# Dividing attention outputs instead of probabilities, in the second and third layer of a fused three-layer kernel

## The reference, cut to what matters

```python
# second layer, per query (256 tokens are one block, so only the own block is seen, causally)
s_own = einsum('bcgrd,bkgd->bcgrk', qc, k_own) * scale
p = masked_softmax(s_own, m_own)          # exp(s - max) / max(sum, 1e-30)
o = einsum('bcgrk,bkgd->bcgrd', p, v_own)
out = (o * silu(z)) @ w_out

# third layer, per block of heads
s = where(valid, q k^T * scale + bias, NEG)
p = softmax(concat([s, sink_col]))[..., :span]      # heads 0-7; heads 8-15 have no sink
o = einsum('bgrqk,bkgd->bqgrd', p, v)
mixed = concat([rms_norm_2(o_a, out_norm_a), rms_norm_2(o_b, out_norm_b)])
x = x + gate1 * (mixed @ w_out)
```

## Time and profile before

| | us |
|---|---|
| median of 3 runs | 1329.05 (1327.18 to 1329.94) |
| the profiled execution | 1329.2 |
| its span in the profile | 1327.9 |
| PE busy / DVE busy / ACT busy in the span | 1263.0 / 1040.0 / 596.9 |

### The profile page before, as it was taken

The page is one execution under the profiler, slowest core; times in us unless marked ns, Lnnn a source line. Parts: engine busy times, 40 slices in busy tenths (PEclk is TensorE's granted clock), DMA queues, the critical chain, the costliest instruction groups (busy, mean ns, idle before and its releaser), DMA issues.

```text
span 1327.9 us, 21963 instructions
## 1 busy us (share of the span) xinstructions
PE 1263.0 (95%) x8283; PEld 1096.5 (83%) x8283; DVE 1040.0 (78%) x2322; ACT 596.9 (45%) x1105; POOL 233.4 (18%) x180
## 2 busy tenths in 40 slices
PE   5988999988999899999999999999999999999997
PEld 5677865676597569999999999999988888888886
DVE  5587896687667878999878888899877777777776
ACT  1434693546342624566554444444443343333432
POOL 0354000360000004688940000000000000000001
PEclk9999999999999989999999999999999999999999
DMA  9877631867578327355544444454566565655553
GB/s 356 294 236 264 240 137 64 291 213 248 186 276 340 112 72 277 136 193 194 175 160 143 159 144 159 144 159 144 161 215 195 191 193 194 196 192 191 193 194 104
DMA packets 92382, 256.82 MB, mean 193 GB/s; under 512 B 9472, under 2 KB 16896, under 8 KB 91904
## 3 DMA queue, kind: packets, MB, share of 16 engines
q1 hardware_dynamic: 59728, 195.91, 44.2%
q10 hardware_dynamic: 32560, 59.66, 12.6%
HBM read 254.47 MB, written 1.06 MB: 192 GB/s over the span
## 4 chain that ended last, share of the span: by engine, by line
PE 72%; DVE 14%; POOL 5%; DMA 3%; ACT 3%; issue 3%; SPq 1%; DVEq 0%; ACTq 0%; POOLq 0%
PE bank L1729 27%; PE bank L1736 26%; PE bank L693 6%; PE bank L2016 4%; PE bank L1123 3%; DVE arena L434 2%; DVE arena L970 2%; PE bank L801 2%; DMA arena<-in_w_in 2%; POOL head_ms L824 2%; DVE u_lo L685 1%; DVE arena L1010 1%; DVE v_lo L685 1%; DMA arena<-in_ada_w 1%; SPq L303 1%
## 5 line engine op out<-in xcount | busy, mean ns | idle before, releaser
L1729 PE MATMUL bank<-h_hi,u_hi 128*128 128x256 f32 x632 | 179.8, 285 | 1.1 <-ACT arena L1854 1.1
L1729 PE MATMUL bank<-h_lo,u_hi 128*128 128x256 f32 x632 | 176.1, 279 | 0.0
L1729 PE MATMUL bank<-h_hi,u_lo 128*128 128x256 f32 x632 | 176.1, 279 | 0.0
L1729 PEld LDWEIGHTS bank<-h_hi,u_hi 128*128 128x128 f32 x632 | 118.8, 188 | 1.3 <-issue 1.3
L1729 PEld LDWEIGHTS bank<-h_hi,u_lo 128*128 128x128 f32 x632 | 119.4, 189 | 0.0
L1729 PEld LDWEIGHTS bank<-h_lo,u_hi 128*128 128x128 f32 x632 | 119.4, 189 | 0.0
L2112 ACT ACTIVATE u_hi<-raw 128x1024 fp32r<-128x1024 f32 x64 | 68.0, 1062 | 104.3 <-PE bank L1736 104.3
L2112 ACT ACTIVATE v_hi<-raw 128x1024 fp32r<-128x1024 f32 x64 | 68.0, 1062 | 101.1 <-PE bank L1736 101.1
L2173 POOL TENSOR_SCALAR raw<-raw 128x1024 f32<-128x1024 f32 x1 | 2.8, 2812 | 624.4 <-DMA raw<-in_final_g 624.4
L1729 PE MATMUL bank<-h_hi,v_hi 128*128 128x256 f32 x392 | 110.9, 283 | 0.0
L434 DVE CUSTOM_DVE_ANT_0 arena<-arena 128x1024 f32<-128x1024 f32 x80 | 102.6, 1295 | 8.6 <-DMA arena<-in_ada_t 7.4
(11 more groups left out here) (277 smaller groups left out, 3431.1 us busy)
## 6 DMA issues: line engine op xcount, KB each, us to landing
raw<-in_u SPq DMA_DIRECT2D x128, 512.0 KB, 3.4
raw<-in_v SPq DMA_DIRECT2D x128, 512.0 KB, 3.6
arena<-in_ada_t SPq DMA_DIRECT2D x80, 512.0 KB, 5.0
arena<-in_ada_w SPq DMA_DIRECT2D x12, 512.0 KB, 12.2
raw<-in_nsa_w_in ACTq DMA_DIRECT2D x3, 2048.0 KB, 11.9
arena<-in_moba_w_in ACTq DMA_DIRECT2D x3, 2048.0 KB, 13.6
arena<-in_w_in ACTq DMA_DIRECT2D x3, 2048.0 KB, 10.4
arena<-in_w_query ACTq DMA_DIRECT2D x3, 2048.0 KB, 10.4
```

Source lines behind the costliest of these rows:

```text
L1729: last = pe.matmul(zbank[k].t[:, 0:S], u[:, c, :], h[:, c, :], start=n == 0, stop=n == 3 * DC - 1)
```

## The change

`attend` gets two arguments, `weigh` and `widened`. Without them (the first layer) the old loop runs, now called `normalised_order`. With them (second and third layer) `normalise` is left out: the exponentials go into the transposes and value products as they are. The reciprocal of each row sum is instead written 64 times side by side, once for each output column of its head (`reciprocals`), transposed on PE like the probabilities into bank 5 (`spread`; two transposes for four heads, four for eight), and multiplied by DVE into the gate or the norm's weights (`weigh`), which the outputs are multiplied by later. The third layer's squares are then of unnormalised outputs, so they are summed for each head (eight products with a 128x2 selector), multiplied by the squared reciprocals and added up (`head_squares`). The order of the loop changes too, and the last pair's `spread` and `outputs` come between the two halves of `tail`.

```diff
+        def reciprocals(p):
+            t, _, lo, hi, _ = pairs[p]
+            rs = rsum[:, t, lo:hi]
+            V.need(m_ex[p])
+            if sink is not None and hi <= sink.shape[1]:
+                V.need(V.did(ve.tensor_tensor(rs, rs, esink[:, t, lo:hi], ALU.add)))
+            V.need(V.did(ve.reciprocal(rs, rs)))
+            V.need(spread_read[0], *widened[1])
+            m_rec[p] = V.did(ve.tensor_scalar(widened[0][:, 0:hi - lo, :], rs.unsqueeze(2).broadcast_to([P, hi - lo, HD]), 1e30, None,
+                                              ALU.min))
+        def spread(p):
+            t, _, lo, hi, _ = pairs[p]
+            b = banks[5]
+            T.need(b.free, m_rec[p])
+            for i in range((hi - lo) // 2):
+                last = pe.transpose(b.t[:, i * P:(i + 1) * P], widened[0][:, 2 * i:2 * i + 2, :].rearrange("p h d -> p (h d)"), ident[:])
+            spread_read[0] = m = T.did(last)
+            V.need(m)
+            b.free = weigh(t, lo // 2, hi // 2, b.t[:, 0:(hi - lo) // 2 * P].rearrange("p (c q) -> p c q", q=P))
...
-                T.need(b.free, m_nm[p, par])
+                T.need(b.free, m_nm[p, par] if weigh is None else m_exp[p, par])
...
+        def weighed_order():
+            for p in range(n + 1):
+                if p < n:
+                    exponentials(p)
+                if p == 1:
+                    fill_wait(fills[0], banks[6])
+                if p + 1 < n:
+                    scores(p + 1)
+                if p == n:
+                    fill_wait(fills[2], banks[3])
+                if p >= 2:
+                    spread(p - 2)
+                if p >= 1:
+                    reciprocals(p - 1)
+                run_later()
+                if p >= 2:
+                    outputs(p - 2)
+                if p == 1:
+                    fill_wait(fills[1], banks[7])
+                if p >= 1:
+                    turned(p - 1)
+                if p < n:
+                    trickle(1)
+                if p == 3:
+                    load_all(loads)
+                pe_us[0] += 3.2
+            tail(range(DC // 2))
+            spread(n - 1)
+            outputs(n - 1)
+            tail(range(DC // 2, DC))
+            run_later()
+            pe_us[0] += 3.2
...
+        def weigh_z(t, lo, hi, spread_out):
+            part = zT[:, lo:hi, t * P:(t + 1) * P]
+            V.need(m_z)
+            return V.did(ve.tensor_tensor(part, spread_out, part, ALU.mult))
...
+        def weigh_norm(t, lo, hi, spread_out):
+            return V.did(ve.tensor_tensor(hT[:, lo:hi, t * P:(t + 1) * P], spread_out,
+                                          norm_cols[:, lo:hi].unsqueeze(2).broadcast_to([P, hi - lo, P]), ALU.mult))
...
-                for c in range(4):
-                    mv = V.did(ve.tensor_scalar(hT[:, 4 * half + c, t * P:(t + 1) * P], bank[:, c, :],
-                                                norm_cols[:, 4 * half + c:4 * half + c + 1], None, ALU.mult))
-                banks[6 + half].free = mv
+                part = hT[:, cs, t * P:(t + 1) * P]
+                banks[6 + half].free = V.did(ve.tensor_tensor(part, bank, part, ALU.mult))
...
-                V.need(squares_read[0])
-                b.free = V.did(ve.tensor_scalar(rstds[:, t, :], b.t[:, 0:2], 1.0 / (HA * HD), EPS, ALU.mult, ALU.add))
+                V.need(squares_read[0], m_rr)
+                b.free = V.did(ve.tensor_tensor(head_squares[:, t, :], b.t[:, 0:NH], rsum_squared[:, t, :], ALU.mult))
+                V.need(b.free)
+                V.need(V.did(ve.tensor_reduce(rstds[:, t, :], head_squares[:, t, :].rearrange("p (a h) -> p a h", a=2), AX, ALU.add)))
+                b.free = V.did(ve.tensor_scalar(rstds[:, t, :], rstds[:, t, :], 1.0 / (HA * HD), EPS, ALU.mult, ALU.add))
```

More of the change, by code:

```diff
@@ L930, in add_outputs, with attend @@
         return inst
-    def attend(branches, q_of, bias_of, first_of, causal_keys, marks, v_marks, begin, done, tail, loads, fills, sink=None):
+    def attend(branches, q_of, bias_of, first_of, causal_keys, marks, v_marks, begin, done, tail, loads, fills, sink=None,
+               weigh=None, widened=None):
         spare_pair[0] = 4
@@ L940, in attend @@
         n = len(pairs)
[L941 removed]
+        m_sc, m_ex, m_nm, m_cp, m_exp, m_rec = {}, {}, {}, {}, {}, {}
+        spread_read = [None]
         def heads(p, par):
@@ L1045, in outputs, with normalised_order @@
             if p + 1 == n or pairs[p + 1][0] != t:
+                if weigh is not None:
+                    V.need(banks[5].free)
                 banks[6].free, banks[7].free = done(t, m)
-        scores(0)
[L1050 to L1076, removed]
+        def normalised_order():
+            for p in range(n + 2):
+                if p < n:
+                    exponentials(p)
+                if 0 <= p - 1 < n:
+                    normalise(p - 1)
+                if p == 1:
[3 more added lines that the diff above has]
+                run_later()
+                if p == n + 1:
+                    tail(range(DC // 2, DC))
+                if p >= n:
+                    fill_wait(fills[2], banks[3])
+                if 0 <= p - 2 < n:
+                    outputs(p - 2)
[3 more added lines that the diff above has]
+                    fill_wait(fills[1], banks[7])
+                if 0 <= p - 1 < n:
+                    turned(p - 1)
+                if p < n and (p or not causal_keys or len(branches) == 1):
+                    trickle(1)
+                if p == 3:
+                    load_all(loads)
+                pe_us[0] += 3.2
@@ L1077, in attend @@
+        scores(0)
+        (normalised_order if weigh is None else weighed_order)()
         spare_pair[0] = 2
@@ L1624, in build @@
         V.need(m_ns)
+        half_of_p = carve([P, 2], s2)
+        m_halves = V.did(ve.tensor_reduce(half_of_p, ident[:].rearrange("p (a n) -> p a n", a=2), AX, ALU.add))
         m_ready = [V.last(), A.last()]
@@ L1680, in build @@
                bias_of, lambda h: nsink[:, h:h + 1] if h < HA else 3e38, False, [*m_ready, *biases.marks], [m_vb], lambda t: None,
-               normed, tail, (query0,), (2, 5, 1), sink=row("sink_a_2"))
+               normed, tail, (query0,), (2, 5, 1), sink=row("sink_a_2"),
+               weigh=weigh_norm, widened=(widened, []))
         run_later(True)
```

36 lines of the change are left out of this document (30 added, 6 removed).

## The result

The changed kernel took 1323.09 us (median of 7, 1320.93 to 1325.50), the kernel before 1330.63 in the same comparison; the ratio is 0.9948 with a 95% interval of 0.9932 to 0.9964, that is 4.8 to 9.0 us faster. One of the seven executions of the kernel before, 2221.39 us, lies far from all others and is not in the ratio. Two later comparisons of the same kernel gave 0.9958 (0.9939 to 0.9977) and 0.9971 (0.9953 to 0.9990). The three together stand for some 5.5 us, where 4.5 had been forecast. The profiled execution took 1322.88 us with a span of 1321.6, 6.3 less than before. Of these 6.3, 4.95 lie between the third layer's first scores and the next projection, 0.8 ahead of the second layer, where nothing was changed, and 0.9 between the second layer's second projection and the third layer's first scores; from that next projection to the end it is 0.3 longer.

The account below looks back on a forecast made before the run. It took no engine as full: PE, DVE and ACT, similarly loaded, wait on one another. 1329.2 - 3.8 (third layer) - 0.75 (second) = 1324.65, by the median 1324.5, stated 1324.6; forecast 1323.2 to 1326.0, range 1321.5 to 1328.0.

Parts of the forecast that it names:

- The third layer's term: Third layer up to L558: earlier turns, products and splits make L558 4.5 earlier; less 0.7, the term is -3.8 us.
- One pair: Third layer's pairs: three DVE instructions of 0.86 replace 1.46 of `normalise`, gaining DVE 0.6; PE gets 0.28 of transposes.
- The floor of 3.45 for PE: Third layer's pairs: PE's work keeps a pair from falling below about 3.45 us, against 3.79 before.
- The DVE wait of 1.96: Third layer's second projection: DVE's wait for PE's chunks disappears if they run at full clock, 1.96 of the 4.5 gain.
- The deduction of 0.7: Boundary of the third layer's halves: a clock fall would cost 1.2, given 0.6, so 0.7 comes off the gain.
- Second layer: Second layer, read at L558: gain 0 at equal clock, 1.5 if the clock drop is avoided; term -0.75 us.
- the one half of 1.5: Second layer: one half given to the new order avoiding the clock drop of 328.60 to 332.00, worth 1.5 us.
- No clock drop at all: Rival, both layers: nothing lost at the boundary, second layer gains 1.5; 1323.2, or 1321.5 at PE's sum; chance 0.12.
- The repeated fall: Rival, pair loops: half clock in two or three pairs loses 1.8 to 2.7 of the gain; 1326.5 to 1328; chance 0.15.
- The rule of the Trainium skill: Counterargument, pairs' banks 4 and 5: pauses from cycling PSUM banks can make the clock swing; cited for the 0.15 rival.
- No effect: Rival: DVE's maxima and the boundary wait set the restart, pairs gain nothing; gain under 1, 1328 to 1330; chance 0.12.
- The ring in bank 5: Rival, every pair: turns' second half waits for `weigh` to free bank 5, some 4.6 us a pair; 1334 total; chance 0.11.

Follow-up runs that it names:

- the runs with the load: Changed kernel with three extra 128x256 DVE multiplications a pair into unread scratch, ahead of the widened write or, later, behind it: ratios to before 1.0003 and 0.9980.
- the runs of the two parts alone: Kernel before with only the last pair moved relative to the chunks: ratio 0.9970; changed kernel with the chunks in their old places: 0.9976.
- the run with the fills: Changed kernel with unread identity products in two PE waits, in the second layer and after the third layer's output projection: ratio to before 0.9953.
- the third layer alone: Changed kernel with the second layer put back to the old order and arithmetic: ratio to before 0.9988.
- the fills with the sums later: Changed kernel with PE waits filled by identity products and the first half's sums of squares one round later in a scores bank: ratio to before 0.9930.

## Why the prediction was right

The forecast of 1324.6, 4.5 us below before, lies within the intervals of the second and third comparison (3.1 to 8.1 and 1.3 to 6.3 us) and 0.3 short of the first's (4.8 to 9.0). The third layer's term and its steps held; the second layer's did not, and about 2 us of the whole have no account. That the total came out near the forecast is in part luck. By its steps:

- **One pair.** DVE gains 0.71 a pair (0.6 forecast): `weigh` 0.34, reciprocal 0.20, widened write 0.21 by differences of starts, 0.75 in place of 0.86. The floor of 3.45 for PE held: from the first to the fifth turns it is 442.43 - 428.58 = 13.85, 3.46 for each of four pairs (3.3 forecast for the first ones). That it is the load of DVE that was removed, and not the wait for its result, the prediction left open; it told the waits on `normalise`, and the runs with the load show that most of what these waits cost was DVE's queue. It counted three waits over half a microsecond where there were four, as the 1.46 at pair 6 was missing from its rows.
- **Third layer.** After the first scores, the first turns come 0.88 earlier (0.7 forecast), pair 4's 2.17 (2.6), pair 5's 1.82 (1.7), products of pair 6 2.25 (2.0), and from there to the sums it takes 10.70 (10.9). L660 comes 3.06 earlier (2.5) and L558 4.96 (4.5). The step from the end of the sums to L660, 473.41 - 472.40, is 1.01 and not 1.1, which changes nothing. The DVE wait of 1.96 went as forecast, and the runs of the two parts alone show that the order of the chunks did it.
- **The clock at the boundary.** The deduction of 0.7 was a chance of a fall, and it came out as such (the 1.2 that it rests on doesn't fit the 0.9 for each group that the rivals use, which would make four groups 3.6; a fall measured about 1.0 here): no fall in the first trace, one in the second, in the run with the fills and in that of the third layer alone, two in the third. Over the four traces of the new third layer without other edits the stretch to the next projection is 72.64 on average, over the two old ones 76.39. That is a gain of 3.75, against -3.8 forecast; with falls that move a single trace by 1 to 2 us, so close a match is luck.
- **Second layer.** This term was wrong in size: -0.75 forecast, nothing measured. The four traces of the new order average 36.95, the two of the old order 36.66; read at L558, as the forecast says, it is 50.97 and 50.87 from the first scores. At equal clock the gain is 0.2 (35.99 to 35.78), as laid out, and the transposes cost 1.9 where 2.2 had been taken. The step that failed is the one half of 1.5 for avoiding the clock's fall. It took the old order's fall as certain, and that order has none in one of its two traces; and the new order has two waits on ACT of its own (1.76 and 1.39) behind which the clock fell, in two of four traces.
- **The rest.** The stretches give -3.5 us, the whole times about -5.5 with intervals of some 2 either way. The difference isn't settled. In the profiled execution 0.8 us had come ahead of the second layer, where nothing was changed, and 0.9 between the layers, of which 0.2 recur in all four traces of the new second layer (17.32 from its second projection to the next transposes, L573, against 17.50 and 17.51 with the old one); among the runs the second layer's first scores started anywhere from 306.37 to 309.49, and from L801 to the end it was 827 to 832 us without any edit there.

**The rivals.** No clock drop at all: seen in no trace of the changed kernel itself, but in that of the fills with the sums later (35.79 and 46.16 at 1.00). The repeated fall: seen in the third execution, which is therefore less of a rival than a part of the spread. The rule of the Trainium skill that was weighed ("TensorE: Matmul & The Clock Gate", section "A second HAM failure mode: psum-queue depth-cycling") speaks of pauses between groups as PE cycles its banks. In the third layer's pairs there are none: PE moves from bank to bank with every group, is busy for 14.87 of 14.87 us, and the clock stays at 1.00. The falls in the two layers stand behind waits for ACT or DVE, of 0.56 to 2.73 us, or behind the small products of the sums, and not behind every one of these; so cycling the banks was not by itself what let the clock fall here. No effect: refuted by the windows and by the three ratios, the lowest of which still leaves 1.3 us. The ring in bank 5: in the changed kernel it shows once, 0.19; with 0.86 us of work a pair more on DVE it shows in both layers (0.61 and 1.04) and most of the pairs' gain goes. Load and ring are not separated there, since the load is what makes `weigh` late.

## What to carry over

Where three engines pass pairs round, read the busy time of each within a window of a few rounds: here DVE had 15.68 of 16.25, then PE 14.87 of 14.87, then, without the transposes, ACT 13.32 of 13.39, and each step ended where the next engine was busy almost throughout. Count the clock's falls before two stretches are compared: a second layer of 35.50 with one fall and 35.79 with none hide a difference of 1.9 us. A wait named after one result may be no more than the queue of the engine that makes it; give the engine its load back without the dependency to tell. And judge a change of a few us by stretches of several traces, since whole executions of the same kernel lay 4.6 to 11.2 us apart within one comparison.

## What had not been expected of the hardware

The granted clock does not follow from the program alone: one sequence with the same instructions and nearly the same waits kept 1.00 behind the boundary (445.47 to 450.52, 5.05 us) in one execution and had 0.74 in another (444.23 to 450.82, 6.59 us), and a fall nearly doubles what follows (turns 1.09 to 1.97, products 1.08 to 1.98). A fall costs nothing where PE then waits for another engine: transposes at 1.97 instead of 1.09 left the next projection where it was, 25.13 us behind the second projection in both executions, since at full clock it waits 1.53 for DVE.
